# RWKV time mix on one core: four f32 projections as f32r parts, in unbroken runs of 24 products

## The reference

```python
xx = token_shift(h) - h
lerp = lambda j: h + xx * mu[j]
xr, xw, xk, xv, xa, xg = (lerp(j) for j in range(N_LERP))
r = xr @ w_in[0]
k = xk @ w_in[1]
v = xv @ w_in[2]
g = xg @ w_in[3]
decay = exp(-exp(-softplus(-(w0 + tanh(xw @ w1) @ w2)) - 0.5))
a = sigmoid(a0 + (xa @ a1) @ a2)
# per token t, per head:
S_t = S_{t-1} diag(w_t) - (S_{t-1} kk_t) (a_t*kk_t)^T + v_t k_t^T ;  y_t = S_t r_t
y = (head_group_norm(y) + bonus) * silu(g)
```

## Time and profile before

| | |
|---|---|
| median of three runs | 4591.2 us |
| profiled execution | 4586.5 us, span 4584.8 us |
| busy share of the span | PE 92%, PEld 70%, DVE 52%, ACT 29%, POOL 6% |
| TensorE clock, mean | 0.938 of full speed |
| first stage, 65.4 to 2165.0 us | PE 2087.7, PEld 1712.4, DVE 1153.1, ACT 636.6, POOL 133.1 us busy, clock 1.00 |
| one step of it | 32.33 us (1015.55 to 1047.88) |

### The profile page before, as it was taken

The page is one execution under the profiler, slowest core; times in us unless marked ns, Lnnn a source line. Parts: engine busy times, 40 slices in busy tenths (PEclk is TensorE's granted clock), DMA queues, the critical chain, the costliest instruction groups (busy, mean ns, idle before and its releaser), DMA issues. The chain is left out here.

```text
span 4584.8 us, 131580 instructions
## 1 busy us (share of the span) xinstructions
PE 4219.0 (92%) x58346; PEld 3217.2 (70%) x58346; DVE 2370.4 (52%) x5302; ACT 1315.9 (29%) x3044; POOL 274.1 (6%) x308
## 2 busy tenths in 40 slices
PE   7999999999999999998988999999969977877579
PEld 5888888888888888886777887888746643444344
DVE  4556555565555655554215543444255533688842
ACT  2233323332323223222213332232113312433221
POOL 1000000000000000000000000000000000111100
PEclk9999999999999999998999999999989988566789
DMA  2322222222222222221413333333211110000010
GB/s 74 92 68 79 63 88 68 83 64 78 77 79 68 79 68 77 70 79 50 127 37 110 96 96 83 101 96 96 55 42 28 23 37 9 1 1 0 0 46 37
DMA packets 520412, 289.54 MB, mean 63 GB/s; under 512 B 30256, under 2 KB 509728, under 8 KB 519904
## 3 DMA queue, kind: packets, MB, share of 16 engines
q1 hardware_dynamic: 519904, 281.88, 21.3%
HBM read 267.55 MB, written 12.58 MB: 61 GB/s over the span
## 5 line engine op out<-in xcount | busy, mean ns | idle before, releaser
L344 PE MATMUL a_bank<-a_lerps,a_wt 128*128 128x256 f32 x4096 | 1036.9, 393 | 2.4 <-DVE a_lerps L815 2.4
L344 PEld LDWEIGHTS a_bank<-a_lerps,a_wt 128*128 128x128 f32 x4096 | 731.0, 189 | 126.9 <-issue 21.2
L1208 PE MATMUL b_bank<-b_hR,b_wR 128*128 128x512 f32 x1024 | 399.8, 390 | 15.5 <-DVE b_wL L1213 15.5
L1208 PE MATMUL b_bank<-b_hL,b_wR 128*128 128x512 f32 x1024 | 399.7, 390 | 0.0
L1208 PE MATMUL b_bank<-b_hR,b_wL 128*128 128x512 f32 x1024 | 399.5, 390 | 0.0
L931 DVE TENSOR_TENSOR a_iv_X<-a_bank,a_iv_X 128x256 f32<-128x256 f32 x256 | 108.7, 425 | 413.3 <-PE a_bank L448 413.3
L1213 DVE TENSOR_TENSOR b_wL<-b_w,b_wR 128x1024 fp32r<-128x1024 f32 (+1 forms) x144 | 192.4, 1340 | 116.8 <-ACT b_wR L1296 104.0
L692 ACT ACTIVATE a_iv<-a_bank 128x512 f32<-128x512 f32 x192 | 114.7, 597 | 419.1 <-PE a_bank L454 266.2
L1208 PEld LDWEIGHTS b_bank<-b_hR,b_wR 128*128 128x128 f32 x1024 | 193.0, 188 | 56.0 <-issue 16.1
L1208 PEld LDWEIGHTS b_bank<-b_hL,b_wR 128*128 128x128 f32 x1024 | 192.9, 188 | 40.4
L1208 PEld LDWEIGHTS b_bank<-b_hR,b_wL 128*128 128x128 f32 x1024 | 193.0, 189 | 40.2
(11 more groups left out here) (441 smaller groups left out, 8156.7 us busy)
## 6 DMA issues: line engine op xcount, KB each, us to landing
a_wt<-in_a_w_in SPq DMA_DIRECT2D x256, 512.0 KB, 4.2
b_w<-in_b_w_in SPq DMA_DIRECT2D x128, 512.0 KB, 4.0
b_w<-in_b_w_out SPq DMA_DIRECT2D x16, 1024.0 KB, 5.6
rwkv_out<-a_ybuf SPq DMA_DIRECT2D x64, 128.0 KB, 5.7
m_w<-in_a_w_out SPq DMA_DIRECT2D x16, 512.0 KB, 4.0
s_wp<-in_w_in SPq DMA_DIRECT2D x12, 512.0 KB, 3.8
a_xtok<-in_x SPq DMA_DIRECT2D x4, 1024.0 KB, 7.1
m_two<-rwkv_out SPq DMA_DIRECT2D x16, 256.0 KB, 3.0
```

Source lines behind the costliest of these rows:

```text
L344: r = mm(o, wt[:, j, c, :], src[:, c, :], start=(c == 0), stop=(c == ND - 1))
L1208: m = nc.tensor.matmul(o, a, b, start=(first and i == 0), stop=(last and i == 2))
```

## The change

Weights and interpolated inputs are each written as a sum of two parts of type f32r: a rounded part (suffix R) and the rest (suffix L). A product becomes three: R by R, R by L of the inputs, L of the weights by R. ACT rounds (`round_weights`, `round_lerp`), POOL subtracts (`low_weights`, `low_lerp`). A projection is then one unbroken run of 24 products, and there are four places for them in a step. Four separate weight tiles and one set of interpolated inputs replace the one weight tile and the double buffer; three small tiles `tmp` pass pairs of interpolated columns from DVE to ACT and POOL. `xx` now lies in the tile of the raw tokens. The diff, cut to its core (the changed order of the PE step follows behind it as lists):

```diff
 def low_rank(m):
...
+                    pe.wait_ge(s["vcp"], m)
+                    mm(bank[1][:, 0:PASS], lwa2[w_rows, :], hwa[w_rows, :], start=True, stop=True)
+                    mm(bank[0][:, 0:PASS], lwa2[a_rows, :], hwa[a_rows, :], start=True, stop=True).then_inc(s["pwa"], 1)
+                def project(o, m, name, lo, hi):
+                    if lo == 0:
+                        pe.wait_ge(s["wL"], m * len(LERPS) + LERPS.index(name) + 1)
+                    if m % NF == 0:
+                        pe.wait_ge(s["lo"], unit(m // NF, name, (hi + 1) // 2 - 1) + 1)
                     for c in range(lo, hi):
-                        r = mm(o, wt[:, j, c, :], src[:, c, :], start=(c == 0), stop=(c == ND - 1))
+                        mm(o, wR[name][:, c, :], lerpR[name][:, c, :], start=(c == 0), stop=False)
+                        mm(o, wR[name][:, c, :], lerpL[name][:, c, :], start=False, stop=False)
+                        r = mm(o, wL[name][:, c, :], lerpR[name][:, c, :], start=False, stop=(c == ND - 1))
...
 ACT
+                def round_weights(m, names=LERPS):
+                    for name in names:
+                        act.wait_ge(s["w" + name], 16 * (m + 1))
+                        sem, count = free(name, 0)
+                        act.wait_ge(s[sem], count + m)
+                        a(wR[name][:, :, :], wt[name][:, :, :], ACT.Copy).then_inc(s["wR"], 1)
+                def round_lerp(ps, name, i):
+                    n = unit(ps, name, i)
+                    act.wait_ge(s["tmp"], n + 1)
...
+                    a(lerpR[name][:, 2 * i:2 * i + 2, :], tmp[n % 3][:, :, :], ACT.Copy).then_inc(s["hi"], 1)
...
+                    lerps(15, ("r", 2), ("r", 3), ("g", 0))
                     if m is not None:
                         decays(m, e)
+                    lerps(15, ("g", 1), ("g", 2), ("g", 3))
...
 POOL
+                def low_weights(m, names=LERPS):
+                    for name in names:
+                        pool.wait_ge(s["wR"], m * len(LERPS) + LERPS.index(name) + 1)
+                        low(wL[name][:, :, :], wt[name][:, :, :], wR[name][:, :, :]).then_inc(s["wL"], 1)
+                def low_lerp(ps, name, i):
+                    n = unit(ps, name, i)
+                    pool.wait_ge(s["hi"], n + 1)
...
+                    low(lerpL[name][:, pair_of, :], tmp[n % 3][:, :, :], lerpR[name][:, pair_of, :]).then_inc(s["lo"], 1)
...
                         root(n - 1)
...
+                    if prep and at == 14:
+                        for name, i in (("k", 0), ("k", 1), ("k", 2), ("k", 3), ("r", 0), ("r", 1)):
+                            low_lerp(prep, name, i)
+                    if prep and at == 15:
+                        for name, i in (("r", 2), ("r", 3), ("g", 0), ("g", 1), ("g", 2), ("g", 3)):
+                            low_lerp(prep, name, i)
+                        for i in range(ND // 2):
+                            low_lerp(prep, "v", i)
                     if m is not None:
+                        if m + 1 < STEPS:
+                            low_weights(m + 1, "krg")
                         bonus(m, pair[1 - par])
+                        if m + 1 < STEPS:
+                            low_weights(m + 1, "v")
+                        if prep and at == 13:
+                            for c in range(ND):
+                                shift(prep, c)
...
 DVE
+                def lerped(ps, *units):
+                    for name, i in units:
+                        n = unit(ps, name, i)
+                        v.wait_ge(s["xx"], ps * ND + 2 * i + 2)
+                        if n >= 3:
+                            v.wait_ge(s["lo"], n - 2)
...
                         scales(n - 1)
                     if m is not None:
                         columns(m, e2, m % NF)
+                    if prep and at == 15:
+                        lerped(prep, ("g", 1), ("g", 2), ("g", 3))
                     add_to_x("X2", "pX2", "X1")
...
                         bonus_keys(m, e2)
+                    if prep and at == 14:
+                        lerped(prep, ("k", 0), ("k", 1), ("k", 2))
+                    if prep and at == 15:
+                        lerped(prep, ("v", 0), ("v", 1), ("v", 2))
...
                     ts(S_all[:, p, :], S4[:, NCH, :], 1.0, None, ALU.mult).then_inc(s["Ssave"], 1)
+                    if prep and at == 14:
+                        lerped(prep, ("r", 2), ("r", 3), ("g", 0))
```

More of the change, by code:

```diff
@@ L170, in rwkv_block @@
         xtok = sb("xtok", [P, PASS // P, D])
-        xx = [sb(f"xx{i}", [P, PASS]) for i in range(2)]
+        xx = xtok[:, :, :].rearrange("p a b -> p (a b)").rearrange("p (c n) -> p c n", n=PASS)
         ybuf = [sb(f"ybuf{i}", [P, PASS]) for i in range(2)]
@@ L413, in first @@
                         turn_x(0, i, 2 + i)
-                    pe.wait_ge(s["wk"], 48)
                     low_in(0, 0, ND, 6)
-                    for c in range(ND):
-                        keys(m, c, c + 1)
                     low_rank(m)
-                    pe.wait_ge(s["lerps"], ND)
-                    gate(m, 0, ND)
-                    receptance(m, 0, ND)
-                    vals(m, 0, ND)
+                    for c in range(0, ND, 2):
+                        keys(m, c, c + 2)
+                    for c in range(0, ND, 2):
+                        receptance(m, c, c + 2)
+                    for c in range(0, ND, 2):
+                        gate(m, c, c + 2)
+                    for c in range(0, ND, 2):
+                        vals(m, c, c + 2)
                     key_norm(m)
@@ L583, in step @@
                     quad(5, pr["P1"], sc["Arb"]).then_inc(s["pR"], 1)
-                    fill(vals, 5, ND)
-                    if prep and at == 14:
-                        low_in(prep, 6, ND)
                     if m is not None:
@@ L746, in _, with low @@
             def _(pool):
+                def low(l, x, rounded):
+                    return nc.gpsimd.tensor_tensor(l, x, rounded.bitcast(F32), ALU.subtract)
                 def bonus(m, e):
@@ L768, in first @@
                         shift(0, c)
+                    for name in LERPS:
+                        low_weights(m, name)
+                        for i in range(ND // 2):
+                            low_lerp(0, name, i)
                     bonus(m, pair[m % 2])
+                    low_weights(m + 1)
                 def root(n):
@@ L881, in first @@
                     columns(m, e, m % NF)
-                    for c in range(ND):
-                        lerped(0, c)
+                    lerped(0, *((LERPS[0], i) for i in range(ND // 2)))
                     rates(m, e)
+                    lerped(0, *((name, i) for name in LERPS[1:] for i in range(ND // 2)))
                     keys(m, e)
```

199 lines of the change are left out of this document (104 added, 95 removed).

## The result

The changed kernel takes 4737.0 us (median of 4 runs, 4719.6 to 4741.4), beside 4591.1 us for the kernel before on the same chip: ratio 1.031, 95% interval 1.0285 to 1.0337. It is slower by 146 us, and the forecast of 4565 us, with its range to 4650, was wrong. The profiled execution took 4719.6 us, span 4717.4. It is the quickest of the four, 17 us under their median, so sums from the trace and differences of medians can differ by that much.

A forecast was written before the change was run, and what follows sets the result against it. PE was taken to bound the kernel before, with POOL's late root holding `normed` after the change. 4586.5 - 142 gained + 116 given back = 4560.5 us profiled; forecast 4565, own range 4500 to 4620, with rivals 4430 to 4650.

The forecast's parts named there:

- PE's own work falls by 4.3 us, to 28.0 us: PE's step: four runs of 24 f32r products at 0.113 us take 11.3 us, replacing 15.6 us of projections.
- `normed` to q, 15.7: PE from `normed` until W0's product is issued (q): 7.25 us other work plus three runs of 2.82 us.
- 7.25 of other work: PE behind `normed`: what remains of the old 16.90 us without five pieces of eight, 9.65 us.
- For a lower clock behind waits of 5 us and more I add 8.: PE's clock after long waits: 8 us added to the time given back.
- The loop over POOL: Root behind four subtractions delays dg: `normed` at q + 14.4, step 30.1 us instead of 32.33.
- Passes: Three changes of pass, steps 13 to 15: loop longer by 22.5 us each, 67 us in all.
- Start: Before the first scores: POOL's subtraction chain moves them from 63.03 to about 87 us, 24 us given back.
- Squares: Steps 8 to 12: ACT's squares and copies delay the roundings, about 5.6 us per pass, 17 us.
- Subtractions: POOL's weight subtractions over 1024 elements: 2.36 us by the row, 2.38 taken for f32r; POOL busy some 800 us.
- Rival 2: Start of a step: port conflicts bring dg a whole subtraction later, q + 16.8; step 32.5 us, 4714 us; chance 0.27.
- Rival 1: PE stays the bound, POOL's root in time: step 28.4 us, total 4435 us; chance 0.2.
- Rival 3: f32r on 256 columns costs as on 512: step at least 38 us, total above 5000; chance 0.03.

The follow-up runs named there:

- experiment 2: Changed kernel, but from the second step's weights on POOL subtracts only one eighth of each weight tile: 4636.4 us, ratio 1.0108.
- experiment 18: Kernel of experiment 1, but S2, E2, S4 and E4 made with 64-wide instead of 32-wide products: 4631.6 us, ratio 1.0100.
- experiment 12: Changed kernel with all its lists, but each projection again 8 f32 products of the rounded parts alone: 4832.3 us, ratio 1.0530.
- experiment 6: Kernel before, with POOL given four useless subtractions over 1024 elements per step: 4589.0 us, ratio 0.9997.
- 17: Kernel before, with each f32 product of 256 columns split into two of 128: 4621.1 us, ratio 1.0069.
- experiment 1: Changed kernel, but POOL subtracts the weights of v behind the next step's root, not in front: 4666.6 us, ratio 1.0166.
- experiment 8: Changed kernel, but for passes 1 to 3 interpolations, their rounding and subtraction work on 32 of 256 columns: 4677.4 us, ratio 1.0196.
- 14: Changed kernel's f32r products in the old PE and ACT order, v's subtraction behind root and dg, DVE subtracting the start's weight tiles: 4633.9 us, ratio 1.0105.
- 15: Kernel of 14, with DVE's copy of the parameter columns in front of X1, no longer behind dg: 4623.3 us, ratio 1.0074.

## Why the prediction was wrong, point by point

- **"PE's own work falls by 4.3 us, to 28.0 us"** (28.2 for the loop) is the step that failed. It is 30.2, by the best step of experiment 2, 29.7 without the waits in it. In the sum it is the term **"`normed` to q, 15.7"**: 18.2 in the mean, 17.8 at full clock. Of the 2.0 us missing in PE's own work, 0.95 are the runs: 3.06 us each, not 2.82. Of these 0.24 us 0.16 is the spacing, 0.1195 us and not 0.113; no row had f32r on 256 columns, and I took the lower of two bounds (the upper was 0.225). The other 0.09 is the change of shape, 0.2 us per run and not 0.11: it was in the earlier trace rows, but I had divided the length of eight instructions by seven starts, of which the first is longer. Before, this cancels (64 x 0.216 + 9 x 0.2 is 15.6 too); after, it doesn't. The other 1.1 is the "7.25 of other work" behind `normed` (8.1 measured, 0.4 of it a hold) and 0.2 in front. Distances between groups in the earlier trace rows had projections between them; that these covered turns from one group to the next fits, but isn't shown by itself.
- **Holds** were not in the sum. In the earlier trace rows there are none to see, since the pieces spread the short instructions. The new order sets some 290 short products in a row, from the scores to X4. They cost 58 us in the stage (72 with the waits for `dg` and others that the profile doesn't name). Behind `normed`, in E8 and X4 alone, they are 0.6 us of an ordinary step at full clock, and 0.01 in experiment 18.
- **"For a lower clock behind waits of 5 us and more I add 8."** The stage ran at 0.96 in the mean: the granted clock has two levels, and from 233.6 to 236.6 us, say, it was 0.50, the lower one (1.2 GHz), behind a hold of 1.43 us that ended at 232.53. PE is busy 30.0 us in a step at full clock, 31.3 in one whose mean is 0.95 and 32.7 at 0.90; in the ordinary steps alone that is 0.45 us a step, 24 us. Such steps came in every kernel whose PE waits, that of experiment 12 with f32 products too, and behind the first step not once in the kernel before or in 6 and 17, whose PE doesn't. Which steps get it the waits in them don't tell: 2.4 us in those at full clock, 2.6 and 2.7 in the others.
- **The loop over POOL.** The order of events was right: `var` and X1 held by v's subtraction, root behind it, `normed` at q + 14.9 (14.4 forecast). But the wait ended last at Arb (65.8 us), before X2's blocks, not at `dg`; E4, S4 and the copy for E8 follow from there. Its worth is 70 us by experiment 1, up to 101 by experiment 2 (51 and 99 by the profiled executions).
- **"`normed` to q, 15.7"** was 17.8 at full clock: 0.72 from the three runs, 0.4 other work, 0.8 to 1.0 holds, most of them in E8 and X4, when ACT's copy of S4 had long been there.
- **Given back.** Passes 67 forecast, 68 measured beyond ordinary steps, and some 45 to 60 of it by size (experiment 8): right. Start 24, 30.3: a little low. Squares 17: in the changed kernel steps 8 to 12 took 0.7 us longer than the other ordinary ones, 0.2 before, so some 8 us more.
- **Subtractions** 2.36 to 2.39 us, POOL 775 us busy in the stage (800 forecast). Right.
- **Rivals.** Rival 2 named nearly the number, a step of 32.5 and 4714 us, and its sign; but its price, `dg` a whole subtraction later at q + 16.8, did not occur. So it was near by luck. Rival 1 fell, and its 28.4 us is below PE's own; yet that PE's own work is most of the step is what it said. Rival 3's price did not occur.

The sum of an ordinary step: 30.2 of PE's own (a hold of 0.4 in it), 0.45 clock, and 2.4 for waits and further holds, which is what is left of 33.05. The forecast had 28.2 and 1.9.

## What to carry to other kernels

Where the bound engine's list is rearranged, its own time has to be rebuilt from rows for each group as it will stand, and where no row has the new instruction, the sum has to be done at both bounds. Here 0.007 us on each of 96 products, 0.09 us at the ends of each run and 1.1 us between groups made 2 of the 3 us by which the step missed. To get an instruction's price and that of a change of shape apart, subtract two pieces of different length. Pieces of long instructions between short ones do two things that no wait shows while they are there: they cover delays on other engines (experiment 6) and they spread the engine's instructions (17 and 18); with instructions half as long the same pieces do the second less well (14 and 15). When a wait is taken away, look at once for what comes next; here a wait of 33 us was worth 11. And a wait without a releaser isn't yet a hold: look whether the instruction waits for a semaphore.

## What the runs showed of the hardware

- With 128x128 weight tiles, at full clock, products start 0.120 us apart for 256 columns of f32r (experiment 2), 0.112 for 128 of f32 (17) and 0.216 for an instruction of 256 of f32.
- PE is held for its own instructions when they are short and dense: 72 us in one kernel at instructions that wait for no semaphore, 20 with 64 fewer products per step (experiments 1 and 18). The Trainium skill (Runtime: NRT & Kernel Launch, "Instruction fetch mechanics") says that instructions come in blocks of 16 KiB and that crossing one is mostly hidden; the trace agrees on the size of a packet, and where 32-wide products stand in a row it isn't hidden, 0.8 us at a time in the mean of experiment 1.
- A DVE instruction on 4 columns, input and output in SBUF, took 2.38 us beside a POOL subtraction of 2.34, and 0.17 in experiment 1, where no subtraction ran; masks that read PSUM kept their 0.41.
